# A two-model fp32 forward pass: conv FFNs fed with unnormalised input and scaled at PSUM, and the modulation's products moved between GpSimd, ScalarE and TensorE

## What is computed

```python
def rmsnorm(x, g):
    y = x * lax.rsqrt(jnp.mean(x * x, axis=-1, keepdims=True) + EPS)
    return y * g

# first model, two layers (i = 0: even_mixer, i = 1: odd_mixer)
h = rmsnorm(x, norm_mix[i])
x = x + mixer(h, w_in, ..., w_out)
x = x + conv_ffn(rmsnorm(x, norm_ffn[i]), w_up, conv_w, conv_b, w_down)

def conv_ffn(h, w_up, conv_w, conv_b, w_down):
    u = h @ w_up                      # 1024 -> 2 x 2816
    u = causal_depthwise_conv3(u, conv_w) + conv_b
    gate, val = jnp.split(u, 2, axis=-1)
    return (silu(gate) * val) @ w_down

# second model, two layers; c is one row of 1024
mod = silu(c) @ w_ada[l] + b_ada[l]   # 6 x 1024 numbers per layer
sh1, sc1, g1, sh2, sc2, g2 = jnp.split(mod, 6, axis=-1)
h = rms_norm(x, ln1_g[l]) * (1 + sc1) + sh1
...
x = x + g2 * (square(relu(h2 @ w_ff1[l])) @ w_ff2[l])
return rms_norm(x, final_g)
```

## Time and profile before

| | |
|---|---|
| median of three executions | 1462.53 us |
| the profiled execution | 1466.21 us |
| its span, first to last instruction | 1464.4 us |
| TensorE busy | 1392.3 us (95%) |
| VectorE, ScalarE, GpSimd busy | 872.1, 802.6, 547.2 us |
| mean granted TensorE clock | 0.974 of full speed |

### The profile page before, as it was taken

The page is one execution under the profiler, slowest core; times in us unless marked ns, Lnnn a source line. Parts: engine busy times, 40 slices in busy tenths (PEclk is TensorE's granted clock), DMA queues, the critical chain, the costliest instruction groups (busy, mean ns, idle before and its releaser), DMA issues.

```text
span 1464.4 us, 25774 instructions
## 1 busy us (share of the span) xinstructions
PE 1392.3 (95%) x11032; PEld 1347.1 (92%) x11032; DVE 872.1 (60%) x1047; ACT 802.6 (55%) x954; POOL 547.2 (37%) x249
## 2 busy tenths in 40 slices
PE   6999899998999979999999998999999999899997
PEld 5989899998999979999988997999988998899996
DVE  4865666755555467666759767434445876734443
ACT  4655577765676457777536544454324554455431
POOL 5000288885331337988606000564000600066300
PEclk9999999999899989999999999999999999999998
DMA  7433677777654466777624444555542543355550
GB/s 261 142 115 115 222 275 261 256 292 305 224 207 159 140 239 241 264 262 269 229 103 170 169 145 144 178 191 179 192 150 80 199 155 144 137 192 190 177 198 29
DMA packets 40002, 278.22 MB, mean 190 GB/s; under 512 B 4432, under 2 KB 4560, under 8 KB 8144
## 3 DMA queue, kind: packets, MB, share of 16 engines
q1 hardware_dynamic: 32976, 226.23, 43.8%
q10 hardware_dynamic: 6912, 50.33, 8.9%
HBM read 275.50 MB, written 1.05 MB: 189 GB/s over the span
## 4 chain that ended last, share of the span: by engine, by line
PE 87%; DVE 6%; ACT 3%; POOL 2%; issue 2%; DMA 0%; DVEq 0%; ACTq 0%; SPq 0%; POOLq 0%
PE bank L738 22%; PE bank L740 22%; PE bank L739 22%; PE bank L703 3%; PE bank L704 2%; PE bank L710 2%; DVE low L1421 2%; PE bank L952 1%; PE bank L722 1%; PE bank L724 1%; PE bank L723 1%; PE bank L772 1%; PE bank L759 1%; DVE h L1554 1%; ACT high L1068 1%
## 5 line engine op out<-in xcount | busy, mean ns | idle before, releaser
L1421 DVE TENSOR_TENSOR low<-raw,high 128x2048 fp32r<-128x2048 f32 (+4 forms) x222 | 510.8, 2304 | 306.0 <-ACT high L1068 303.7
L738 PE MATMUL bank<-op_high,low 128*128 128x256 f32 x1904 | 549.1, 288 | 3.3 <-DVE low L1421 3.3
L739 PE MATMUL bank<-op_low,high 128*128 128x256 f32 x1904 | 540.5, 284 | 0.0
L740 PE MATMUL bank<-op_high,high 128*128 128x256 f32 x1904 | 540.4, 284 | 0.0
L1068 ACT ACTIVATE high<-raw 128x2048 fp32r<-128x2048 f32 (+4 forms) x222 | 406.3, 1831 | 155.2 <-PE bank L740 143.6
L738 PEld LDWEIGHTS bank<-op_high,low 128*128 128x128 f32 x1904 | 367.4, 193 | 8.8 <-DVE low L1421 4.4
L739 PEld LDWEIGHTS bank<-op_low,high 128*128 128x128 f32 x1904 | 367.3, 193 | 2.8 <-issue 2.4
L740 PEld LDWEIGHTS bank<-op_high,high 128*128 128x128 f32 x1904 | 367.1, 193 | 0.0
L738 PE MATMUL bank<-act_high,low 128*128 128x256 f32 x864 | 242.7, 281 | 0.0
L740 PE MATMUL bank<-act_high,high 128*128 128x256 f32 x864 | 242.0, 280 | 0.0
L739 PE MATMUL bank<-act_low,high 128*128 128x256 f32 x864 | 240.6, 278 | 0.0
(11 more groups left out here) (288 smaller groups left out, 1910.6 us busy)
## 6 DMA issues: line engine op xcount, KB each, us to landing
raw<-stream SPq DMA_DIRECT2D x198, 1024.0 KB, 4.8
adaw<-ada ACTq DMA_DIRECT2D x48, 1024.0 KB, 6.2
raw<-stream SPq DMA_DIRECT2D x10, 768.0 KB, 4.5
raw<-stream SPq DMA_DIRECT2D x10, 512.0 KB, 3.6
x<-xT SPq DMA_DIRECT2D x1, 1024.0 KB, 5.1
out<-h SPq DMA_DIRECT2D x1, 1024.0 KB, 3.9
raw<-stream SPq DMA_DIRECT2D x2, 384.0 KB, 3.3
consts<-consts_d SPq DMA_DIRECT2D x1, 672.0 KB, 14.1
```

The costliest lines, as they stand in the source:

```text
L738: pe.matmul(o, wl[:, w], oh[:, k, :], start=one, stop=False, skip_group_check=True)
L739: pe.matmul(o, wh[:, w], ol[:, k, :], start=False, stop=False, skip_group_check=True)
L740: mm = pe.matmul(o, wh[:, w], oh[:, k, :], start=False, stop=end, skip_group_check=True)
L1421: dve.tensor_tensor(low[m % SPLIT][:, 0:w], raw[m % RAW][:, 0:w], high[m % SPLIT][:, 0:w], ALU.subtract).then_inc(S["low_ready"], 1)
```

## The change

1. **Conv FFNs on x times the weight.** Chunks named in `DEFERRED` (all 44 up chunks, bq0, bk0, od000, od001) take as operand x times the norm's weight, without rn. ScalarE writes its high part and VectorE its low part, pair by pair, in a new stage `xg` right after the squares. The last sum of squares goes into the middle of the first such chunk (`FIRST`), ahead of its third pair. The product is scaled by rn in a new VectorE instruction that reads PSUM and writes to SBUF (`scaled_to`, parts of `h`), and what used to read PSUM (L1110, L1493, the squares of the units) reads that SBUF tile.
2. **The convolution is one chunk later** in the order (`conv`, after the next chunk's scaling), and `gate`/`val` are rings of three.
3. **The split of the chunk three further on** comes, at the last chunk of a projection before norms 1 to 3, after the x updates and `xg`. The three splits at the start come before norm 0, and the small products `ar` and `la` later.
4. **Modulation.** The host lays the weights out transposed, so that a partition holds an output and the free dimension the inputs. c is broadcast to a tile `crow` (128 x 1024). GpSimd multiplies each of the two blocks by `crow` in place, and ScalarE, two steps later, sums each along its row with a copy that has `accum_out`. `ada_sum` and `adas` are gone.
5. Constants are loaded after the first weight chunk, and the gains by a DMA of their own.

```diff
+        DEFERRED = {"bq0": 0, "bk0": 0, "od000": 2, "od001": 2}
+        DEFERRED.update({f"up{l}{v}{j}": 2 * l + 1 for l in range(2) for v in "gv" for j in range(11)})
+        def scaled_to(name):
+            if name in ("bq0", "bk0"):
+                return Sb[name == "bq0"][:]
+            at = 2 * (int(name[4]) if name.startswith("od") else (2 * int(name[4:]) + (name[3] == "v")) % 4)
+            return h[:, at:at + 2, :]
...
         def conv_stages(l):
-            st_("norm", 2 * l + 1), st_("ffn_in", l)
+            st_("norm", 2 * l + 1)
...
             for j in range(11):
                 for half in "gv":
-                    c(f"up{l}{half}{j}")
-                    if half == "g" and j:
-                        st_("act", (l, j - 1))
+                    name = f"up{l}{half}{j}"
+                    c(name, split=False)
+                    if taken is not None:
+                        st_("conv", taken)
+                    high_low(name), st_("conv_init", name)
                     if half == "v":
+                        if j:
+                            st_("act", (l, j - 1))
                         st_("silu", (l, j))
+                    taken = name
                     modulation()
...
 # TensorE, in the first chunk after a norm
+                        if name in FIRST and at == 4:
+                            if name == "bq0":
+                                sumsq((0, 2))
+                            sumsq((FIRST[name], 3))
...
-            def ada_sum(seg):
-                pe.wait_ge(S["ada_added"], 4 * (seg + 1))
...
 # ScalarE
+            def xg(a):
...
+                for k in (2 * p, 2 * p + 1):
+                    ins = act.activation(XG_HIGH[i][:, k, :], x[:, k, :], ACT.Copy, scale=gains[i][:, k:k + 1])
+                ins.then_inc(S["xg_high"], 1)
...
+            def ada_acc(a):
...
                 for i in range(2):
-                    k = 2 * (a % 4) + i
-                    ins = act.activation(adaw[a % 3][:, i, :], adaw[a % 3][:, i, :], ACT.Copy, scale=cact[:, k:k + 1])
-                ins.then_inc(S["ada_scaled"], 1)
+                    act.wait_ge(S["ada_scaled"], 2 * a + i + 1)
+                    m = 8 * part + 2 * q + i
+                    act.activation(w[:, i, :], w[:, i, :], ACT.Copy, accum_out=mod[:, l, m:m + 1])\
+                        .then_inc(S["ada_summed"], 1)
...
 # VectorE
+            def xg(a):
...
+                for k in (2 * p, 2 * p + 1):
+                    ins = dve.scalar_tensor_tensor(out=XG_LOW[i][:, k, :], in0=x[:, k, :], scalar=gains[i][:, k:k + 1],
+                                                   in1=XG_HIGH[i][:, k, :], op0=ALU.mult, op1=ALU.subtract)
...
+                if name in DEFERRED:
+                    dve.wait_ge(S["rstd_ready"], DEFERRED[name] + 1)
+                    dve.wait_ge(S["products_done"], n + 1)
+                    dve.tensor_tensor(scaled_to(name), ps[b][:], rn[:].rearrange("p (a b) -> p a b", a=1)
+                                      .to_broadcast([P, 2, TOK]), ALU.mult).then_inc(S["first_scaled"], 1)
...
+            def conv(name):
+                l, j, v = int(name[2]), int(name[4:]), int(name[3] == "v")
+                dst, src = (cg, cv)[v][j % CONV], scaled_to(name)
...
+                        ins = dve.scalar_tensor_tensor(out=dst[:, i, d:], in0=src[:, i, 0:TOK - d],
+                                                       scalar=col("conv", t + tap, 1), in1=dst[:, i, d:],
+                                                       op0=ALU.mult, op1=ALU.add)
...
 # GpSimd
             def ada_(a):
...
-                pool.wait_ge(S["ada_added"], a)
-                link(pool.tensor_tensor(acc[:], w[:, 0, :], acc[:], ALU.add))
-                pool.tensor_tensor(acc[:], w[:, 1, :], acc[:], ALU.add).then_inc(S["ada_added"], 1)
...
+                for i in range(2):
+                    pool.tensor_tensor(w[:, i, :], w[:, i, :], crow[:], ALU.mult).then_inc(S["ada_scaled"], 1)
```

More of the change, by code:

```diff
@@ L34 @@
 AX = mybir.AxisListType
-RAW, SPLIT, RELU = 3, 3, 3
+RAW, SPLIT, RELU, CONV = 3, 3, 3, 3
 CHUNK = 2048
@@ L277, in build @@
         AL = f("act_low", [P, 22, TOK], F32R)
-        cg = [f(f"gate{i}", [P, 2, TOK]) for i in range(2)]
-        cv = [f(f"val{i}", [P, 2, TOK]) for i in range(2)]
+        cg = [f(f"gate{i}", [P, 2, TOK]) for i in range(CONV)]
+        cv = [f(f"val{i}", [P, 2, TOK]) for i in range(CONV)]
         ffn.close()
@@ L390, in projection @@
             for n, name in enumerate(names):
-                c(name)
+                final = i in XG_HIGH and n + 1 == len(names)
+                c(name, split=not final)
                 if pair > behind:
@@ L534, in build @@
                 done = BY[i]["n"]
-            elif stage == "norm" and i:
+            elif stage == "norm" and i not in XG_HIGH:
                 BEFORE_NORM[i] = done
@@ L758, in sumsq @@
                 for k in (2 * p, 2 * p + 1):
-                    mm = pe.matmul(ps[NB][:, 0, :], col("ones"), h[:, k, :], start=not i and k == 0, stop=k == KB - 1)
+                    mm = pe.matmul(ps[NB][:, 0, :], col("ones"), h[:, k, :], start=False, stop=k == KB - 1)
                 if p == 3:
@@ L1538, in norm @@
             def norm(i):
+                if i not in NORMED_AT:
+                    return
                 if i < 4:
-                    g = col("norm_mix" if i % 2 == 0 else "norm_ffn", 8 * (i // 2), 8)
-                    shift = None
+                    g, shift = gains[i], None
                 elif i < 8:
@@ L1806, in mla_p @@
                         .then_inc(S["att_low"], 1)
-            stages = dict(chunk=chunk, low=low_after, square_add=square_add, norm=norm, late=late, unit=unit, lam=lam, la=la_, la_exps=la_exps, gla_att=gla_att,
+            stages = dict(chunk=chunk, conv=conv, low=low_after, xg=xg, first_split=first_split, square_add=square_add, norm=norm, late=late, unit=unit, lam=lam, la=la_, la_exps=la_exps, gla_att=gla_att,
                           gla_kv=gla_kv, gated=gated, mix=mix, diff_s=diff_s, diff_w=diff_w, dil_s=dil_s,
```

286 lines of the change are left out of this document (163 added, 123 removed).

## The result

The changed kernel takes 1542.05 us (median of four runs, 1540.24 to 1543.9), the kernel before 1464.61 us beside it; the ratio is 1.0532 [1.0507, 1.0557]. It is slower by 77 us where I had forecast 28.5, and above my range. The profiled execution took 1540.24 us, its span 1538.4.

The account below looks back on a forecast made before the run. TensorE, busy 95% of the span, bounds the kernel. Gains 14.5 + 6.0 + 8.0 + 4.5 + 2.5 = 35.5 us against a loss of 64 give +28.5: 1462.5 + 28.5 = 1491 us, range 1461 to 1526.

Parts of the forecast that it names:

- the up chunks: Rounds of a pair: VectorE and GpSimd exclude each other, 15.3 us against 11.5, a loss of 32 us per stage.
- norm 2: Deferring norm 2 shortens 14.8 us to 7.0, a gain of 8 us if od010 finds its normalised operand.
- The twelve sums: L952's modulation sums leave TensorE, 1.68 us each; the seven outside the up chunks plus idle time gain 14.5 us.
- rival A: Up chunks: convs don't exclude GpSimd, TensorE sets the pace, gains of 44 us, 1419 us; chance 0.12.
- Rival B: Up stages: TensorE, waiting, gets 1.2 GHz for parts, +30 to +50 us, 1520 to 1540 us; chance 0.07.
- Norms 1 and 3: Deferral shortens TensorE's gaps there: 6.0 us gained at norm 1, 4.5 at norm 3 (bounds 0 and 7).
- that work is now under 11 us of two chunks; it just fits: Norm 2: VectorE's some 6.4 us for od010's normalised operand fits under two chunks; the gain of 8 us needs this.
- Case C: Norms and start: gap stays, `xg` being late in queues; 6 of 21 us remain, 1506 us; chance within the forecast's 0.74.
- Both stay under TensorE outside the up chunks: Outside the up chunks ScalarE (+19 us, hidden in idle time) and GpSimd (96 multiplications for 84 additions) stay under TensorE.
- The start: TensorE's first chunk starts at 15.6 us instead of 24.04, a gain of 2.5 us (bounds 0 and 5).

Follow-up runs that it names:

- e1: The changed kernel with the up chunks' products scaled in place in PSUM, so the convs read PSUM again; 1491.1 us, ratio 1.0182 to the kernel before.
- e5: e1 with norm 2 as before the change (od000 and od001 take the normalised operand); 1487.53 us, ratio 1.0144 to the kernel before.
- e2: The changed kernel with GpSimd's 96 multiplications replaced by short fills, so the modulation isn't computed; 1433.16 us, ratio 0.9784 to the kernel before.
- e4: The kernel before with only the modulation's part of the change, norms and convs as before; 1469.58 us, ratio 1.0028 to the kernel before.
- e10: The changed kernel without the 28 multiplications of the down chunks, so the modulation isn't computed; 1522.63 us, ratio 1.0381 to the kernel before.
- e12: e5 with modulation parts moved: 9 among each stage's up chunks, 8 and 7 among down chunks, 15 beside odd chunks; 1480.84 us, ratio 1.0114.

## Why the prediction was right and wrong

The direction, the mechanism in the up chunks and their size were right. The total was wrong, because the same exclusion was given no price in the down chunks and norm 2 was given a gain that it didn't have.

The forecast by its own terms, between the x updates of the table. The twelve sums are put where before's trace has them, at 1.68 us each, those of the up chunks within the 32; the last 2.7 us of idle time are not placed. The sums at 513.93 and 734.61 start behind the products of odo0 and down1_3, so they count in the stretches after those.

| stretch | forecast | measured |
|---|---|---|
| start to evo3 | -2.5 | +0.8 |
| norm 1, up chunks, first down chunks | -6.0 + 32 = +26.0 | +28.9 |
| down0_0 to down0_3 | -3.4 | +9.2 |
| norm 2 and odd chunks to odo0 | -8.0 - 3.4 = -11.4 | -3.6 |
| odo0 to odo3 | -1.7 | +2.2 |
| norm 3 and up chunks | -4.5 + 32 = +27.5 | +28.8 |
| down1_0 to down1_3 | -1.7 | +4.9 |
| rest of the kernel | -1.7 | +2.8 |

The measured terms sum to 74.0, the difference of the two profiled executions (1540.24 and 1466.2); the forecast's to 31.2, less 2.7. Of the 45.5 us between them 19.2 lie in the two stages of down chunks and 7.8 at norm 2.

*The up chunks: right.* Mechanism, round (15.0 for 15.3) and the sum of both stages came nearly as worked out, and rival A fell with the changed kernel's own trace and with e1: a conv does hold GpSimd off. TensorE was busy 84% of the two rounds from 250.5 to 280.5, not about 75%. Rival B fell too: in 180 to 290 us the mean granted clock of the changed kernel is 0.97, its TensorE busy 94.65 of 110 us, and from 200 on it stands waiting for a `low` once in every round, so the clock isn't what costs.

*Norms 1 and 3: right.* The first up chunk's product, which ScalarE first read at 166.08, is scaled at 160.34 in the changed kernel, at the end of TensorE's wait:

```profile
153.39 0.69 DVE L1533 TENSOR_TENSOR x<-bank,x 128x512 f32<-128x512 f32 x1
...
160.34 0.69 DVE L1547 TENSOR_TENSOR h<-bank,rn 128x512 f32<-128x512 f32 x1 [0.54 <-PE bank L761]
```

From the end of the x update to this scaling are 6.3 us, where before took 12.8 to ScalarE's first read: 6.6 us gained for 6.0. At norm 3 the x update ends at 567.65 and the scaling starts at 576.54, 8.9 us, against 14.2 in before (530.16 to 544.32): 5.3 for 4.5.

*Norm 2: wrong by about 8.* The step "that work is now under 11 us of two chunks; it just fits" failed. The products of od000 and od001 come in time, but their units (the squares, sums and scaling that each such product of the odd mixer gets for its own small norm) need them scaled by VectorE, and that instruction stands in its queue behind all of the norm's (VectorE, GpSimd, ScalarE and TensorE of the changed kernel):

```profile
405.37 1.67 DVE L1638 SCALAR_TENSOR_TENSOR h<-x,params,rn 128x256 f32<-128x256 f32 x4 [1.05 <-ACT rn L1245]
...
411.84 3.43 DVE L1496 TENSOR_TENSOR odd_low<-h,odd_high 128x512 fp32r<-128x512 f32 x2
415.20 0.68 DVE L1547 TENSOR_TENSOR h<-bank,rn 128x512 f32<-128x512 f32 x1
```
```profile
415.91 0.63 ACT L1115 ACTIVATE sq<-h 128x512 f32<-128x512 f32 x1 [3.33 <-DVE h L1547]
```
```profile
416.59 2.08 PE L824 MATMUL bank<-sq,consts 128*128 128x512 f32 x2 [7.46 <-ACT sq L1115]
```

So the gap that went from the product came back 7.46 us long one unit later. The scaling stands last in that queue, and GpSimd's multiplications stretched the queue from the 6.4 us that I had counted to 9.8 (405.37 to 415.20); the 3.43 us for two short subtractions are part of it. Case C named a late queue, but looked at `xg` and not at the scaling. e5 shows that the deferral costs more than it brings. In e2, where no multiplication is in the way, it gains 1.4 us between down0_3 and the first unit and 4.0 to the second, still half of the 8.

*"Both stay under TensorE outside the up chunks": wrong by 19 us.* This is the largest miss: +9.2 and +4.9 in the down chunks where I had -3.4 and -1.7, and perhaps part of the 2.9 us in the stretch ahead of them. That sentence compares the engines' work with TensorE's time and gives no price to the exclusion there. It leaves out that the old additions were held back by ScalarE and the new multiplications aren't, that the deferral of norm 2 adds two instructions for each x update (`xg`) to VectorE in the first down chunks, and that `mod` now reads SBUF. e4, which has the new modulation and no `xg`, loses 4.8 and 5.6 us in the two stages; the other 4.4 of the first stage are about what `xg` costs by e5 (4.7). e10 gives 19.4 us back, 13.6 of them in the first stage and 4.2 in the second by the x updates. The price of such a wait stood in the earlier trace rows, for four norm products; I had applied it to the up chunks alone.

*The start: wrong by 3.* The first matmul came when forecast (15.56 us for 15.6), but the lead was gone by evo3. By the prediction's own terms, 8.4 less 5.3 and 1.7, the gain is 1.4 and not 2.5. That the rest lay in the first chunks' units, which wait for their scaled products, is an idea from the traces and no run tested it; single executions differ there by as much.

*Two slips in the rivals.* Rival B takes a quarter of the two stages as 20 chunks; of 44 up chunks it is 11, so its price should have been some 26 us and not 30 to 50. Rival A's breaking point, a round of 13.9, is reached with convs that hold GpSimd off for 0.28 us, not 0.30. Neither moves the forecast.

*What the square adds.* The losses aren't additive: the modulation's price (4, 21, 38 us) depends on how much VectorE and GpSimd already exclude each other. A forecast that priced each edit alone would have come out at 4 + 40 = 44 us by the ratios; 78 are there. That fits one shared resource that was nearly full before (11.7 us in a round of 11.5).

Open: what pacing alone is worth in the down chunks, e12's loss in the second down chunks, the start, and the 2.8 us behind the first model.

## What to carry to other kernels

Before moving an operand of a VectorE instruction from PSUM to SBUF, add up for each round what VectorE does with two SBUF operands and all that GpSimd does; if the sum is near the round, each microsecond more is a microsecond lost, and an engine's low busy share says nothing of it. Do the same sum outside the stage that you changed. Count a freed wait as a possible cost too: what it had held back now runs in a block, and the short instructions of the other engine stand behind long ones. A product computed early gains nothing if the instruction that scales it is queued behind the work that it was to overtake.

## What was new about the hardware

The wait doesn't depend on the waiting instruction's size: 8 columns (0.16 us) took 2.36 us, 256 columns (0.42) 2.63, 1536 columns (1.76) 3.63. They paid 2.2, 2.2 and 1.9 us, nearly the whole of one GpSimd instruction of 1024 columns (2.35). After it GpSimd's next one waited in turn, so the two engines mostly alternate one by one, and ten multiplications (23.5 us) took 33.68. Whether the waiting pair is a multiplication or an addition on GpSimd makes no difference (four convs: 6.39 and 6.40 us). The same addition of 8 columns with one operand in PSUM took 0.16 us beside a running GpSimd instruction. From this I read that many short instructions against few long ones is the worst mix, since the number of VectorE's instructions in a busy stretch sets the price, up to the number of GpSimd's; no run varied that number alone. And the price of GpSimd's width had a bend: 33 us for the first half, 76 for the second.
